# A decoder layer on one core: when the last expert's weights are fetched, and how the final norm is spread over the engines

## The reference

```
h = h + Mixer(RMSNorm(h))
h = h + CrossAttn(RMSNorm(h), memory K/V)
h = h + HierMoE(RMSNorm(h))          # top-1 group of 4, then top-2 of its 8 experts
y = RMSNorm_final(h)

def rms_norm(x, g):
    y = x * lax.rsqrt(jnp.mean(x * x, axis=-1, keepdims=True) + RMS_EPS)
    return y * g

def expert_block(args):              # 32 experts, D_EXPERT 512
    xi, e = args
    h = jax.nn.silu(xi @ w_eg[e]) * (xi @ w_eu[e])
    return h @ w_ed[e]
```

## Time and profile before

| | us |
|---|---|
| Median of 3 runs (2322.73 to 2330.76) | 2323.11 |
| The profiled execution | 2317.78 |
| Its span, first to last instruction | 2316.1 |
| PE busy | 2104.0 |
| DVE busy | 599.5 |
| ACT busy | 472.4 |
| POOL busy | 258.4 |

### The profile page before, as it was taken

How to read it: one execution, slowest core, us unless ns; L and a number is a source line. 1 busy time by engine, 2 the same in 40 slices (tenths; PEclk the granted TensorE clock), 3 DMA queues, 4 the chain that set the end, 5 groups by cost and what they waited for, 6 DMA issues and landing times.

```text
span 2316.1 us, 33699 instructions
## 1 busy us (share of the span) xinstructions
PE 2104.0 (91%) x12706; PEld 1186.5 (51%) x12706; DVE 599.5 (26%) x1416; ACT 472.4 (20%) x1013; POOL 258.4 (11%) x402
## 2 busy tenths in 40 slices
PE   6999998999969999999999999898599999999971
PEld 4577765666635665666665446646333333333320
DVE  4221224666610140111111020622511111111116
ACT  3212223444410000000000021403122222212112
POOL 1001222322221000000000000000011111111110
PEclk9999999999979999999999999997799999999995
DMA  8356778887894124002002120400989999999946
GB/s 313 106 156 215 248 268 280 288 263 260 256 335 137 37 82 146 1 1 73 1 0 82 37 87 1 155 1 33 351 300 377 383 375 368 375 373 372 372 186 230
DMA packets 193546, 458.65 MB, mean 198 GB/s; under 512 B 18465, under 2 KB 27698, under 8 KB 193258
## 3 DMA queue, kind: packets, MB, share of 16 engines
q1 hardware_dynamic: 161306, 360.06, 43.9%
q0 software_dynamic: 32080, 96.44, 12.3%
HBM read 432.51 MB, written 32.17 MB: 201 GB/s over the span
## 4 chain that ended last, share of the span: by engine, by line
PE 81%; DMA 7%; DVE 4%; issue 3%; SPq 2%; ACT 2%; DVEq 1%; POOLq 0%; ACTq 0%; POOL 0%
PE ps L886 19%; PE ps L1288 10%; PE ps L895 7%; PE ps L1319 5%; PE ps L1147 5%; PE ps L1299 5%; PE ps L913 5%; PE ps L1013 4%; PE ps L1217 3%; PE ps L1328 2%; DMA kraw<-in_cache_k 2%; PE ps L928 2%; PE ps L1049 2%; PE ps L1024 2%; PE ps L962 2%
## 5 line engine op out<-in xcount | busy, mean ns | idle before, releaser
L886 PE MATMUL ps<-xnT,ring 128*128 128x352 f32 x1536 | 468.4, 462 | 3.5 <-DMA ring<-in_w_in 2.6
L886 PEld LDWEIGHTS ps<-xnT,ring 128*128 128x128 f32 x1536 | 292.3, 191 | 173.2 <-issue 10.2
L1288 PE MATMUL ps<-gu,xgT 128*64 128x512 f32 x1024 | 228.4, 599 | 12.6 <-DMA wd<-in_w_expert_down 11.7
L2307 POOL DMA_DIRECT2D vpage<-in_cache_v x256 | 137.5, 537 | 435.6 <-issue 426.7
L1013 PE MATMUL ps<-consts,kraw 128*128 128x128 f32 x1024 | 141.4, 283 | 29.3 <-DMA kraw<-in_cache_k 18.7
L1013 PEld LDWEIGHTS ps<-consts,kraw 128*128 128x128 f32 x1024 | 115.3, 144 | 62.1 <-issue 30.3
L1288 PEld LDWEIGHTS ps<-gu,xgT 128*64 128x64 f32 x1024 | 71.4, 138 | 144.6 <-issue 141.5
L1840 DVE COPY kt<-ps 128x512 f32<-128x512 f32 x128 | 88.4, 691 | 185.1 <-PE ps L1013 184.4
L1319 PE MATMUL ps<-wd,hidT_a 128*64 128x512 f32 x512 | 118.6, 605 | 18.3 <-ACT hidT_a L1601 12.3
L895 PE MATMUL ps<-ring,mixT 128*128 128x512 f32 (+1 forms) x288 | 124.0, 593 | 1.3 <-DVE mixT L1982 1.3
L1299 PE MATMUL ps<-gu,xgT 128*32 128x512 f32 x1024 | 115.8, 592 | 0.0
(11 more groups left out here) (341 smaller groups left out, 2386.4 us busy)
## 6 DMA issues: line engine op xcount, KB each, us to landing
kraw<-in_cache_k SPq DMA_DIRECT2D x256, 256.0 KB, 3.7
vpage<-in_cache_v POOLq DMA_DIRECT2D x256, 256.0 KB, 4.7
gu<-in_w_expert_gate SPq DMA_DIRECT2D x32, 2048.0 KB, 20.1
gu<-in_w_expert_up SPq DMA_DIRECT2D x32, 2048.0 KB, 24.8
wd<-in_w_expert_down SPq DMA_DIRECT2D x32, 2048.0 KB, 21.2
ring<-in_w_in SPq DMA_DIRECT2D x7, 2048.0 KB, 9.7
yy<-y_d SPq DMA_DIRECT2D x16, 512.0 KB, 11.4
early<-in_w_in SPq DMA_DIRECT2D x6, 1024.0 KB, 10.6
```

The source lines that it names most:

```text
L886: last = nc.tensor.matmul(bank(R.bank(*tag))[:, 0:NC_], slot[:, k, f * P:(f + 1) * P], xnT[:, k, cols_of(n)], start=k == 0, stop=k == KD - 1)
L1288: last = nc.tensor.matmul(bank(0)[h * BA:(h + 1) * BA, :].rearrange("p (x n) -> p x n", x=2), src[:, k, 0:BA], weight[:, k, :, h * DE // 2 ...
L2307: pool.dma_start(vpage[n % VS][:, p, :], t["cache_v"][ds(page, 1)].rearrange("a s d -> (a s) d")).then_inc(v_in[n % VS], 16)
```

## The change

It does four things.

1. Gate and up weights of expert 31 wait only for gb_e of expert 28; the wait for db of expert 29 is taken out of L846. In SP's loop a wait for a new semaphore, more_down_free, stands between the gate and up loads and the down load. ACT raises it once, when it has seen db of expert 29, and POOL raises it after each trip, beside more_free.
2. The transposes of a trip's rows and the copy to xgT move from the end of the trip before (for expert 31: from the unrolled loop of expert 30) to the start of the trip. The gather for expert 31 counts on more_xg_in.
3. The final norm goes tile by tile. ACT: square with row sum, then the root with scale 1/D and the epsilon as bias from a small tile epsc (set once by DVE at the start). DVE: the reciprocal, after the sum of the next tile. ACT: resid times the reciprocal root, in place. POOL: resid times the gain, in place.
4. SP stores straight from resid, and waits for all nine stores on one semaphore.

```diff
-            R.made(sp, "gb_e", LAST - GUS), R.made(sp, "db", LAST - WDS)
+            R.made(sp, "gb_e", LAST - GUS)
...
                     sp.dma_start(gu[LAST % GUS][:, :, x, :], expert_load(j, which)).then_inc(more_w_in, 16)
+                sp.wait_ge(more_down_free, j)
+                apart(sp)
                 sp.dma_start(wd[LAST % WDS], expert_load(j, "w_expert_down")).then_inc(more_w_in, 16)
...
-                sp.wait_ge(n_fin.scaled, i + 1)
+                sp.wait_ge(fin_scaled, i + 1)
                 dst = t["y_prompt"][i * P:(i + 1) * P, :] if i < PT else t["y_sample"]
-                sp.dma_start(dst, xf[i % 4][0:rows_of(i), :]).then_inc(y_out[i % 4], 16)
-            for p in range(4):
-                sp.wait_ge(y_out[p], 16 * (3 if p == 0 else 2))
+                sp.dma_start(dst, resid[0:rows_of(i), i, :]).then_inc(y_out, 16)
+            sp.wait_ge(y_out, 16 * TILES)
...
-                else:
-                    pe.wait_ge(xg_in[LAST % 2], 16 * (LAST // 2 + 1))
-                    R.read(pe, "xt_e", e)
-                    turn_rows(xg[LAST % 2]).then_inc(more_pe, 1)
...
             with pe.Fori(1, n) as j:
+                pe.wait_ge(more_xg_in, j * 16)
+                apart(pe)
+                turn_rows(xg[LAST % 2]).then_inc(more_pe, 1)
                 pe.wait_ge(more_w_in, j * 48)
...
-                pe.wait_ge(more_xg_in, j * 16)
-                apart(pe)
-                turn_rows(xg[LAST % 2]).then_inc(more_pe, 1)
...
+                if e == LAST - WDS:
+                    act.sem_inc(more_down_free, 1)
...
-                else:
-                    R.made(act, "gb_e", LAST - 2)
-                    act.wait_ge(more_pe, 1)
-                    copy_rows(xgT[LAST % 2]).then_inc(more_act, 1)
...
+            R.made(act, "gb_e", LAST - 2)
             with act.Fori(1, n) as j:
+                act.wait_ge(more_pe, j * 7 - 6)
+                copy_rows(xgT[LAST % 2]).then_inc(more_act, 1)
...
-                act.wait_ge(more_pe, j * 7 + 1)
-                copy_rows(xgT[LAST % 2]).then_inc(more_act, 1)
-            n_fin.act_stats(act, lambda i: resid[:, i, :], lambda i: act.wait_ge(summed, i + 1))
+            def norm_rows(i):
+                r = rows_of(i)
+                act.wait_ge(fin_ready, i + 1)
+                nc.scalar.activation(resid[0:r, i, :], resid[0:r, i, :], ACT.Copy, scale=ss[0:r, 5, i:i + 1]).then_inc(fin_normed, 1)
+
+            for i in range(TILES):
+                r = rows_of(i)
+                act.wait_ge(summed, i + 1)
+                nc.scalar.activation(junk[0:r, :], resid[0:r, i, :], ACT.Square, accum_out=ss[0:r, 4, i:i + 1])
+                act.drain()
+                nc.scalar.activation(ss[:, 5, i:i + 1], ss[:, 4, i:i + 1], ACT.Sqrt, scale=1.0 / D, bias=epsc).then_inc(fin_root, 1)
+                if i:
+                    norm_rows(i - 1)
+            norm_rows(TILES - 1)
...
+            nc.vector.memset(epsc, EPS)
...
+            def invert_root(i):
+                dve.wait_ge(fin_root, i + 1)
+                nc.vector.reciprocal(ss[:, 5, i:i + 1], ss[:, 5, i:i + 1]).then_inc(fin_ready, 1)
...
+                if i:
+                    invert_root(i - 1)
+            invert_root(TILES - 1)
-            n_fin.dve_scale(dve, lambda i: resid[:, i, :], 5, lambda i: dve.wait_ge(y_out[i % 4], 16 * (i // 4 + 1)))
...
-            pool.wait_ge(xg_in[LAST % 2], 16 * (LAST // 2 + 1))
-            pool.wait_ge(more_pe, 1)
...
                 pool.sem_inc(more_free, 1)
+                pool.sem_inc(more_down_free, 1)
...
-            pool.wait_ge(more_xg_in, last * 16)
+            pool.wait_ge(more_xg_in, last * 16 + 16)
             apart(pool)
+            pool.wait_ge(gain_in, 16 * 5)
+            for i in range(TILES):
+                r = rows_of(i)
+                pool.wait_ge(fin_normed, i + 1)
+                nc.gpsimd.tensor_tensor(resid[0:r, i, :], resid[0:r, i, :], gain[0:r, :], ALU.mult).then_inc(fin_scaled, 1)
```

More of the change, by code:

```diff
@@ L181, in build_program @@
         ones = new("ones", [P, 1])
+        epsc = new("epsc", [P, 1])
         pages = new("pages", [1, DB * PAGES], I32)
@@ L406, in build_program @@
                              "odd_y_ready"))
-        more_w_in, more_list_in, more_xg_in, more_y_out, more_free, more_pe, more_act, more_dve = (
-            sem(n) for n in ("more_w_in", "more_list_in", "more_xg_in", "more_y_out", "more_free", "more_pe", "more_act",
-                             "more_dve"))
+        more_w_in, more_list_in, more_xg_in, more_y_out, more_free, more_down_free, more_pe, more_act, more_dve = (
+            sem(n) for n in ("more_w_in", "more_list_in", "more_xg_in", "more_y_out", "more_free", "more_down_free", "more_pe",
+                             "more_act", "more_dve"))
         summed = sem("summed")
-        y_out = [sem(f"y_out{p}") for p in range(4)]
+        y_out, fin_root, fin_ready, fin_normed, fin_scaled = (
+            sem(n) for n in ("y_out", "fin_root", "fin_ready", "fin_normed", "fin_scaled"))
         R = Results(sem("result_full"), sem("read_by_act"), sem("read_by_dve"))
@@ L642, in build_program @@
         n_mix, n_mem = Norm("nmix", 0, TILES, [(0, 2), (2, 5), (5, TILES)]), Norm("nmem", 1, 2)
-        n_xat, n_ffn, n_fin = Norm("nxat", 2, TILES, bufs=xf), Norm("nffn", 3, TILES, bufs=xf), Norm("nfin", 4, TILES, [(0, PT), (PT, TILES)], xf)
+        n_xat, n_ffn = Norm("nxat", 2, TILES, bufs=xf), Norm("nffn", 3, TILES, bufs=xf)
         ring_xo = ring[0].rearrange("p k n -> p (k n)").rearrange("p (k n) -> p k n", k=KC)
@@ L2360, in expert_gather @@
                         R.made(pool, "xt_e", LAST - 2)
-                gather(xg[e % 2], lists[0:BLK, 0, e:e + 1]).then_inc(xg_in[e % 2], 16)
+                gather(xg[e % 2], lists[0:BLK, 0, e:e + 1]).then_inc(xg_in[e % 2] if e < LAST else more_xg_in, 16)
             def expert_scatter_b(e):
```

## The result

| | before | after |
|---|---|---|
| Median of 20 runs each, us | 2322.88 | 2330.06 |
| Ratio, 95% interval | | 1.0032 (1.0019 to 1.0044) |
| Span of the profiled execution | 2316.1 | 2335.3 |
| First piece | 36.57 | 30.62 |
| Second piece | 45.5 | 60.2 |

The change makes the kernel 7.2 us slower. I forecast +0.6, which is 6.6 too little. The change stays within 0.5%, and 2330.06 lies just above the upper end of my range (2330). Piece times come from one profiled execution of each kernel; that of after is the longest of its 20 (2336.97), that of before was one of its shorter ones (2317.78).

A forecast was written before the change was run, and what follows sets the result against it. TensorE, busy 91% of the span, was taken as the bound, except at the end. Weights -9.1 and norm +9.7 net +0.6 us on the 2323.11 median: 2323.7, range 2308.5 to 2330.

The forecast's parts named there:

- Weights half, -9.1: Before the last expert: earlier weight loads start its first product 7.5 us earlier, plus 1.6 from a held clock; -9.1 us.
- I take the clock as held, 1.6 us more: Expert 31's first product on PE: granted clock stays up after the shorter pause, 7.09 us instead of 8.69.
- My bound: Gap before the last expert: gain of only 7.5 us if PE's clock falls all the same.
- Norm half, +9.7: Final norm: DVE's sums and POOL's products, both reading two SBUF tiles, take turns; end 2325.8, +9.7 us; chance 0.55.
- the store 2327.7: End of the norm: last store under turn-taking at 2327.7, before 1.9 us off for overlapped start-up gave end 2325.8.
- side by side: Rival, final norm: DVE and POOL work on tiles together undisturbed; norm -3.0, net -12.1 us, 2311; chance 0.27.
- slow POOL: Rival, final norm: POOL's product costs over 3.8 us per tile; +12 to +20 us, 2338; chance 0.08.
- gap 4.2 around the transposes: Sign, before the last expert: PE's gap, transposes within it, is 4.2 us.
- first product 7.1: Sign, last expert: its first product on PE is 7.1 us long.
- sums of tiles 3 to 8 well over 1.28: Sign, final norm: mean DVE sum well over 1.28 us, two or more near 3.5, means turns; 1.28 throughout means overlap.
- POOL near 2.5: Sign, final norm: POOL's product takes near 2.5 us per tile; under 1.5 or over 3.8 would be wrong.
- last sum to end near 10: Sign, final norm: from DVE's last sum to the kernel's end takes near 10 us, against 14.6 before.

The follow-up runs named there:

- transposes ahead: Kernel before with only early gate/up loads and the separate wait for down; transposes stay in expert 30's part: 2312.75 us against 2325.05, ratio 0.9950.
- sum from PSUM: Whole change, but the sums' third operand comes from an unused PSUM bank, leaving the sum itself out: 2317.11 us (one run) against 2323.56 before.
- POOL stays: Kernel before plus one wait: POOL ends its list only after DVE's last norm product; no tile work added: 2332.25 us (one run) against 2323.56.
- norm half: Kernel before with only the tile-by-tile norm and direct stores (parts 3 and 4): 2346.84 us against 2323.56, ratio 1.0106.
- fewer copies: As "combined", but ACT copies only tiles 2 to 7 to PSUM: 2302.68 us against 2323.00 for the kernel before, ratio 0.9918.
- combined: Change reworked: transposes ahead, PE's register load before its waits, full tiles' sums through PSUM, POOL multiplying tiles 0 to 4 only: 2308.38 us against 2323.51 before, 0.9941.
- weights half: Kernel before with only early weights and moved transposes (parts 1 and 2), old norm: 2317.58 us against 2323.56, ratio 0.9973.

## Why the prediction failed where it did

The time fell outside my range because of one term that I had put at nothing, POOL's closing drain. In order of the sum:

**Weights half, -9.1, measured -6.0 in the first piece.** The mechanism held: no load was late, and the down weights were issued at 2234.21 with the DMA idle by about 2242 (share 0.02 in 2242 to 2244), some 7 us before the first product, which waits for them. The entry was forecast at 4.2 us and took 4.68, so the start gained 7.05 instead of 7.5. The step that failed in this half is "I take the clock as held, 1.6 us more": the clock fell just before the product, which took 9.77 instead of 7.09, so the term was +1.1 instead of -1.6. My bound (-7.5 if the clock falls all the same) was too narrow as well: it assumed that a product at a fallen clock would still take the 8.69 of before, while it took 8.63 to 9.96 in nine of the ten executions that start it early. By the granted clock of the stretches (0.86 in 2254 to 2256) the change's product ran slow to about 2254.6, for 5.4 us; that of before to about 2249.0 (0.75 in the second line here), for 3.3, because its clock had fallen long before it began:
```profile
2246.00:2248.00 2.00, 2.00 (x6) 0.56 (x5) 0.00 (x0) 0.00 (x0) 0.00 (x0) 0.50 0.00 0
2248.00:2250.00 2.00, 2.00 (x10) 0.64 (x8) 0.00 (x0) 0.00 (x0) 0.00 (x0) 0.75 0.00 0
```
Half of each is what the product lost: 2.7 and 1.6 us. That the moved transposes cost openly was right: 1.6 forecast, 1.9 to 2.4 measured (4.68 and 5.2 from PE's end to the product, and 2.80 in "transposes ahead").

**Norm half, +9.7: the mechanism was right.** DVE and POOL take turns, as "sum from PSUM" shows. The sizes: POOL's product is 2.33 alone, not 2.57, and a pass and a product together take 3.3 us where 1.28 + 2.33 in sequence would be 3.6, so about 0.3 of each pair does overlap (0.2 was my estimate). And not all of it was turns: ten sums were left when POOL began, where I had twelve, seven of them were slow, and POOL rested twice for 3.7 us, waiting for ACT, which waited for a slow sum. I expected the last store 55.2 us after the first fetch; it was in at 52.1. The term for this half, but for the drain, was 3.1 too large. *The estimate of 2.25 us from the Trainium skill, page "GPSIMD Engine Reference", section on elementwise cycle accounting, was nearer to POOL's time than mine.*

**What the sum had no term for: +8.1. This is the step that failed.** The prediction ends its sum with "the store 2327.7": "end" was for me the last store. POOL's drain of 10.03 us was in the trace of before at 2286.2, hidden by 20 us of other work, and was not among my rows. I asked for each queue what the change moves past it, but not what POOL still has to do after its last instruction. Moving nine products behind that work took the cover away. "POOL stays" shows the price with no product moved: +7.3.

So +0.6 became +8.8 by the pieces: +3.1 from the weights, -3.1 from the turns, +8.1 from the drain, +0.1 from rounding. That the first two misses cancel is luck; the drain is what is left. The rival "side by side" (-12.1) fell, "slow POOL" (over 3.8 us a tile) too. The marks that I had named read as follows: gap 4.2 around the transposes (4.68), first product 7.1 (9.77, wrong), sums of tiles 3 to 8 well over 1.28 (seven of the twelve at 3.2, mean 2.46, right), POOL near 2.5 (2.33 to 3.3, right), last sum to end near 10 (2317.70 to 2335.3, 17.6, wrong by the drain).

What stays open: why the clock fell in one execution of a kernel and not in the other after the same pause, and what exactly POOL's drain waits for, or settles.

## What to carry to other kernels

Before work is moved to an engine at the end of a kernel, look at what that engine's closing drain costs and what hides it now; POOL's took 10 us after its own scatters and gathers, and a chain that counts only stores does not have it. An idle engine is no free engine: ask what its operands share with the neighbour's, and count two passes with two SBUF inputs, one on DVE and one on POOL, as one after the other (3.3 us for a pair here, where 3.6 is the sum). And when a load is released earlier, leave the small work that its wait used to hide where another wait still hides it.

## What was not expected of the hardware

- POOL's drain: 10034 ns to the nanosecond in seven kernels whose POOL was idle by then, whether issued at 2277 or at 2320; in the change, where products were still running, it ended 10.06 us after the last.
- POOL's product takes 2.33 us for the tile of 32 partitions as for one of 128.
- ACT's scaling of a tile in place took 1.13 us, its square of the same tile 1.04 to 1.06.
- TensorE's granted clock fell in one execution after a pause of 1.98 us and held in another after one of 1.99.
- POOL's gather of the rows took 1.03 us to issue in some kernels and 1.6 to 2.0 in others (1.88 in the norm half, 1.96 in "fewer copies") in the same place beside the sums. I had noted it as undisturbed by them. It was 1.03 in both kernels whose sums there read PSUM ("sum from PSUM", "combined"), and 1.6 to 2.0 in nine of the eleven executions whose sums read two tiles from SBUF; the other two (before, weights half) had 1.03. So the sums' second SBUF input seems to reach the gather as well, though no experiment isolates it.
